# Five of six late transpose groups of a one-core trunk layer: VectorE's 32x32 blocks and a round trip through memory in place of TensorE

## The reference

```python
mod = c_act @ w_ada[l] + b_ada[l]
shift, scale, gate = jnp.split(mod, 3, axis=-1)
h = rms_norm(x, norm_g[l]) * (1 + scale[:, None]) + shift[:, None]
proj = h @ w_in[l]
...
y_pool = multiscale_pool(pool_u, pool_w[l], pool_scale[l]) * jax.nn.silu(pool_z)
y_attn = window_attention(...) * jax.nn.silu(attn_z)
y_conv = conformer_conv(conv_a, conv_b, ..., conv_pw[l]) * jax.nn.silu(conv_z)
g_pool, g_attn, g_conv = jnp.split(jax.nn.sigmoid(gates), 3, axis=-1)
merged = (g_pool * (y_pool @ w_branch_pool[l])
          + g_attn * (y_attn @ w_branch_attn[l])
          + g_conv * (y_conv @ w_branch_conv[l]))
x = x + gate[:, None] * (merged @ w_out[l])
return rms_norm(x, final_g)
```

## Time and profile before

| | |
|---|---|
| median of the runs | 943.31 us |
| span of the profiled execution | 941.5 us |
| PE busy | 910.7 us, 97% of the span |
| DVE busy | 702.5 us, 75% |
| ACT busy | 420.3 us, 45% |
| POOL busy | 9.2 us, 1% |
| HBM read, written | 217.24 MB, 2.10 MB |

### The profile page before, as it was taken

How to read it: one execution, slowest core, us unless ns; L and a number is a source line. 1 busy time by engine, 2 the same in 40 slices (tenths; PEclk the granted TensorE clock), 3 DMA queues, 4 the chain that set the end, 5 groups by cost and what they waited for, 6 DMA issues and landing times.

```text
span 941.5 us, 10294 instructions
## 1 busy us (share of the span) xinstructions
PE 910.7 (97%) x4211; PEld 732.5 (78%) x4211; DVE 702.5 (75%) x793; ACT 420.3 (45%) x387; POOL 9.2 (1%) x26
## 2 busy tenths in 40 slices
PE   1999999999999999999999999999999999999996
PEld 1668677888888888888877777888888888888885
DVE  4768796878968777767778786685687988865783
ACT  3435252645344334444375655447434443444332
POOL 2000000000000000000000000000000000000000
PEclk9999999999999999999999999999999999999999
DMA  9999999855446556555545456657879998965512
GB/s 339 387 387 386 374 328 387 317 182 179 150 161 208 198 181 200 201 179 179 181 136 175 138 157 148 207 172 155 267 242 396 374 335 275 352 209 190 182 45 89
DMA packets 108207, 220.01 MB, mean 234 GB/s; under 512 B 3857, under 2 KB 3937, under 8 KB 107392
## 3 DMA queue, kind: packets, MB, share of 16 engines
q1 hardware_dynamic: 106768, 213.15, 66.6%
q0 software_dynamic: 1104, 5.42, 1.5%
q10 hardware_dynamic: 288, 0.79, 0.2%
HBM read 217.24 MB, written 2.10 MB: 233 GB/s over the span
## 4 chain that ended last, share of the span: by engine, by line
PE 87%; DVE 5%; DMA 4%; ACT 2%; issue 1%; SPq 0%; DVEq 0%; ACTq 0%
PE acc_odd L1245 12%; PE acc_odd L1247 12%; PE acc_odd L1246 12%; PE acc_even L1245 12%; PE acc_even L1247 12%; PE acc_even L1246 12%; DMA raw<-in_w_in 2%; PE side_a L1245 2%; PE side_a L1247 2%; PE side_a L1246 2%; DVE gate_sums L1088 1%; DMA x_tok<-in_x 1%; PE side_b L1294 1%; DVE ada_sums L804 1%; DVE wl L758 1%
## 5 line engine op out<-in xcount | busy, mean ns | idle before, releaser
L758 DVE TENSOR_TENSOR wl<-raw,wh 128x2048 fp32r<-128x2048 f32 x148 | 338.2, 2289 | 148.3 <-ACT wh L466 147.9
L466 ACT ACTIVATE wh<-raw 128x2048 fp32r<-128x2048 f32 x148 | 282.0, 1913 | 263.9 <-PE acc_odd L1247 105.5
L1245 PE MATMUL acc_even<-wh,act_h 128*128 128x512 f32 x432 | 170.5, 395 | 0.6 <-DVE act_l L853 0.6
L1245 PE MATMUL acc_odd<-wh,act_h 128*128 128x512 f32 x432 | 169.8, 393 | 0.0
L1247 PE MATMUL acc_even<-wh,act_l 128*128 128x512 f32 x432 | 168.3, 390 | 0.0
L1246 PE MATMUL acc_odd<-wl,act_h 128*128 128x512 f32 x432 | 168.2, 389 | 0.0
L1247 PE MATMUL acc_odd<-wh,act_l 128*128 128x512 f32 x432 | 168.2, 389 | 0.0
L1246 PE MATMUL acc_even<-wl,act_h 128*128 128x512 f32 x432 | 168.2, 389 | 0.0
L973 DVE SCALAR_TENSOR_TENSOR conv_slots<-conv_slots,taps 128x256 f32<-128x256 f32 x240 | 100.2, 478 | 0.2
L1245 PEld LDWEIGHTS acc_even<-wh,act_h 128*128 128x128 f32 x432 | 81.1, 188 | 20.5 <-issue 3.8
L1245 PEld LDWEIGHTS acc_odd<-wh,act_h 128*128 128x128 f32 x432 | 81.1, 188 | 18.9 <-issue 2.2
(11 more groups left out here) (288 smaller groups left out, 916.8 us busy)
## 6 DMA issues: line engine op xcount, KB each, us to landing
raw<-in_w_in SPq DMA_DIRECT2D x106, 1024.0 KB, 5.1
raw<-in_w_ada SPq DMA_DIRECT2D x48, 1024.0 KB, 8.9
raw<-in_w_out SPq DMA_DIRECT2D x16, 1024.0 KB, 5.0
raw<-in_w_branch_pool SPq DMA_DIRECT2D x8, 1024.0 KB, 5.0
raw<-in_w_branch_attn SPq DMA_DIRECT2D x16, 512.0 KB, 6.7
raw<-in_w_branch_conv SPq DMA_DIRECT2D x8, 1024.0 KB, 6.5
raw<-in_conv_pw SPq DMA_DIRECT2D x4, 1024.0 KB, 6.6
x_tok<-in_x SPq DMA_DIRECT2D x2, 1024.0 KB, 9.0
```

The lines of the kernel that those rows point to most:

```text
L466: nc.scalar.activation(wh[:, m % RING], raw[SLOT_OF[g]][:, :, :], ACT.Copy).then_inc(high_done, 1)
L758: nc.vector.tensor_tensor(wl[:, m % RING], raw[SLOT_OF[load_of(m)]][:, :, :], wh[:, m % RING].bitcast(F32), ALU.subtract).then_inc(raw_don ...
L1245: nc.tensor.matmul(sums, xh, wh[:, slot, i, :], start=begin, stop=False)
```

## The change

Five groups leave PE: both of `zs_conv` and the first three of `merged`. For each, `turn_blocks` on DVE transposes the 32x32 blocks inside each partition quadrant with two instructions of 512 columns, into one of two `blocks` buffers. POOL's `turn` then writes the group to DRAM with four DMAs (one for each quadrant of 32 partitions, 128 KB in 1024 pieces of 128 bytes, 512 bytes apart), waits until all four have landed, and reads it back with two DMAs of 256 KB in rows of 2 KB, into the place where the group came from. ACT's spread and DVE's low_halves then read that place in place of a PSUM bank. The sixth group, `merged` 3, is still turned on PE at m = 137.

What else moves: the spreads of `zs_conv` from m = 111 and 113 to 115 and 116, their low halves from 112 and 114 to 116 and 117; the spread of `merged` 2 from 135 to 136 and its low half to 137; the additions to `gate_rows` from 116 to 121 for the first; the gate row's PSUM place alternates between the two halves of `pa`, so PE waits for the addition before the last one only. On POOL, x_res comes after the first two turns, gate_rows waits for the second low half, and final_rows comes after the last turn, since it lies over `blocks`. Transposes on VectorE and writes to DRAM of such short pieces do not occur in the kernel before.

```diff
--- before.py
+++ after.py
@@ constants and buffers @@
+TURNS = 5
...
+    blocks = [at(f"blocks{s}", [P, 4, 4, TH, QUAD], F32, (176 + 4 * s) * KB) for s in range(2)]
+    scratch = [nc.dram_tensor(f"turned_{g}", (QUAD, 4, 4 * TH, 4, QUAD), F32, kind="Internal").ap() for g in range(TURNS)]
...
+        def turned_tiles(g):
+            return by_channels(g) if g >= 2 else zs_conv[g][:, :, :].rearrange("p h (t s) -> p (h t) s", t=2)
...
+        def by_channels(g):
+            if g < 2:
+                return zs_conv[g][:, :, :].rearrange("p h c -> p (h c)").rearrange("p (q t s) -> p q t s", q=2, t=2)
+            return merged[:, :, bass.ts(g - 2, COLS)].rearrange("p q (t s) -> p q t s", t=2)
@@ gpsimd @@
-            pool.wait_ge(used, END["pw1"])
+            def turn(g):
+
+                pool.wait_ge(blocks_ready, g + 1)
+                for a_ in range(4):
+                    pool.dma_start(scratch[g].rearrange("j b n a i -> j (b n) a i")[:, :, a_, :],
+                                   blocks[g % 2][QUAD * a_:QUAD * (a_ + 1), :, :, :, :].rearrange("j b t h i -> j (b t h) i")
+                                   ).then_inc(blocks_stored, 16)
+                pool.wait_ge(blocks_stored, 16 * 4 * (g + 1))
+                rows = scratch[g].rearrange("j b (q n) a i -> q b j (n a i)", q=2)
+                for q in range(2):
+                    pool.dma_start(by_channels(g)[:, q, :, :].rearrange("p t s -> p (t s)"), rows[q]
+                                   ).then_inc(turned[g], 16)
+
+            turn(0)
+            turn(1)
             pool.dma_start(x_res[:, :, :], x_rows).then_inc(x_res_loaded, 16)
-            pool.dma_start(final_rows[:, :], a["final_g"].partition_broadcast(P)).then_inc(final_loaded, 16)
-            pool.wait_ge(y_t, 4)
+            pool.wait_ge(y_ready, 6)
             pool.dma_start(gate_rows[:, :], a["b_ada"][0, 2 * D_MODEL:3 * D_MODEL].partition_broadcast(P)
                            ).then_inc(gate_b_loaded, 16)
+            for g in range(2, TURNS):
+                turn(g)
+            pool.dma_start(final_rows[:, :], a["final_g"].partition_broadcast(P)).then_inc(final_loaded, 16)
@@ scalar @@
-                if m in (111, 113):
-                    b = (m - 111) // 2
-                    spread(y_h[:, 4 * b:4 * b + 4, :], by_tiles((pa, pb)[b]), y_t, 3 + b, y_high)
+                if m in (115, 116):
+                    b = m - 115
+                    spread(y_h[:, 4 * b:4 * b + 4, :], turned_tiles(b), turned[b], 16 * 2, y_high)
...
-                if m in (131, 133, 135, 137):
-                    j = (m - 131) // 2
-                    spread(act_h[:, 4 * j:4 * j + 4, :], by_tiles((pb, pb, pa, pb)[j]), y_t, 5 + j, y_high)
+                if m in (131, 133, 136):
+                    j = (131, 133, 136).index(m)
+                    act.wait_ge(used, END["gc3"])
+                    spread(high_tiles(j), turned_tiles(2 + j), turned[2 + j], 16 * 2, y_high)
+                if m == 137:
+                    spread(act_h[:, 12:16, :], by_tiles(pb), y_t, 3, y_high)
@@ vector @@
+            def turn_blocks(g, src):
+
+                for h in range(TH):
+                    last = nc.vector.transpose(blocks[g % 2][:, :, :, h, :].rearrange("p b t i -> p t b i"),
+                                               src[:, h, :].rearrange("p (t b j) -> p t b j", t=4, b=4))
+                last.then_inc(blocks_ready, 1)
...
-                if m in (112, 114):
-                    b = (m - 112) // 2
-                    low_halves(5 + b, y_h[:, 4 * b:4 * b + 4, :], y_l[:, 4 * b:4 * b + 4, :], (pa, pb)[b])
+                if m == 112:
+                    for b in range(2):
+                        dve.wait_ge(*freed(f"pw{b}"))
+                        turn_blocks(b, zs_conv[b][:, :, :])
+                if m in (116, 117):
+                    b = m - 116
+                    low_halves(5 + b, y_h[:, 4 * b:4 * b + 4, :], y_l[:, 4 * b:4 * b + 4, :], turned_tiles(b))
+                if m in (122, 124, 134):
+                    j = (122, 124, 134).index(m)
+                    dve.wait_ge(merged_ready, 9 + j)
+                    turn_blocks(2 + j, merged[:, :, bass.ts(j, COLS)])
...
-                if m in (116, 122, 128, 134):
-                    q = (m - 116) // 6
+                if m in (121, 122, 128, 134):
+                    q = (121, 122, 128, 134).index(m)
...
-                if m in (131, 133, 135, 137):
-                    j = (m - 131) // 2
-                    tiles = slice(4 * j, 4 * j + 4)
-                    low_halves(7 + j, act_h[:, tiles, :], act_l[:, tiles, :], (pb, pb, pa, pb)[j])
+                if m in (131, 133, 137):
+                    j = (131, 133, 137).index(m)
+                    low_halves(7 + j, high_tiles(j), low_tiles(j), turned_tiles(2 + j))
+                if m == 137:
+                    low_halves(10, act_h[:, 12:16, :], act_l[:, 12:16, :], by_tiles(pb))
@@ tensor @@
-                if m in (111, 113):
-                    b = (m - 111) // 2
-                    pe.wait_ge(*freed(f"pw{b}"))
-                    if b:
-                        pe.wait_ge(y_ready, 4)
-                    else:
-                        pe.wait_ge(var_ready, 2)
-                    transpose4((pa, pb)[b], block_of(zs_conv[b]), y_t)
                 if m in (114, 120, 126, 132):
                     q = (m - 114) // 6
                     pe.wait_ge(sums_low, q + 1)
...
-                if m in (131, 133, 135, 137):
-                    j = (m - 131) // 2
-                    pe.wait_ge(merged_ready, 9 + j)
...
-                    transpose4((pb, pb, pa, pb)[j], block_of(merged, COLS * j), y_t)
+                if m == 137:
+                    pe.wait_ge(merged_ready, 12)
+                    pe.wait_ge(y_ready, 4)
+                    transpose4(pb, block_of(merged, COLS * 3), y_t)
```

30 lines of the change are left out of this document (16 added, 14 removed).

## The result

The changed kernel takes **968.85 us** (median of 4 runs, 967.50 to 971.56), the kernel before 943.25 beside it: ratio 1.0273, 95% interval 1.0261 to 1.0285, 25.6 us slower. The forecast was 955.8 (946.5 to 980). The profiled execution took 967.5.

A forecast was written before the change was run, and what follows sets the result against it. PE was taken as the bound, busy 910.7 of 941.5 us. The terms 0 + 6.2 + 2.8 - 2.6 + 6.1 gave +12.5 us on 943.3, so 955.8 us, range 946.5 to 980.

The forecast's parts named there:

- (c): DMA, m = 112 to 120: full engines, short write pieces at three times their bytes' time; second gate row +6.2 us.
- (e): Last turned group, o0's third piece: write phase 9.6, reads 4.4, then 6.6 to the operand; PE stands for 6.1 us.
- (a): On PE's path: five transpose groups leave, 5 x 0.88 = 4.4 us; first two lie ahead of the first gate row.
- (b): DVE at m = 112: four transposes add 2.6 us, `gate_low` starts as before, PE waits 1.8 longer; net 0.
- (d): DVE between gate rows, m = 120 and 126: transposes and moved addition delay third `gate_low`, +2.8 us; later DMAs cost nothing.
- (f): Moved x_res (some 40 us later) and final_rows: cost nothing, hidden by o0; SP's queue not touched, only its bandwidth.
- sum of the low bounds: Whole kernel: every term at its low bound but (b), +3.8 - 0.9, given as about +4 us.
- short-piece rival: Round-trip writes: 1024 pieces take pool_w's time whatever their bytes, 16 us a group; +27, 970.6 us; chance 0.33.

The follow-up runs named there:

- tiny: Changed kernel with the round trip's DMAs cut to a quarter of their bytes each way, most turned values left out: 951.90 us.
- tinyx: Changed kernel with the round trip's DMAs cut to a quarter of their bytes each way and x_res loaded behind the last turn: 944.56 us.
- xlate: Changed kernel with the load of x_res moved behind the last turn, just ahead of final_rows: 966.88 us.
- long2: Changed kernel with the round trip's writes in pieces of 4 KB in place of 128 bytes, values ending at other places: 964.89 us.
- reads16: Changed kernel with each group's read-back cut into four DMAs by partitions in place of two by halves: 966.94 us.
- both5: Changed kernel with read-backs in four DMAs by partitions and x_res loaded behind the last turn: 958.05 us.

## Why the prediction was right and wrong

The sign and the place of the waits were right, and the time lay in the range; the size was half of what came. Most of the miss is in (c), in (e) and in a term for the clock that the sum doesn't have.

(a), (b) *Right.* PE lost the groups; a transpose took 0.65 from start to start as taken, the first gate row waits 1.4 (forecast 1.8), net -0.7 for 0; the gate sums came 1.9 earlier (711.52 for 713.44) where I took 1.5.

(c) **The step that failed**, by its size and by its reason. +9.3 for +6.2. I had put it on the short pieces of the writes, at three times their bytes. Long pieces change this stretch by nothing (42.9 for 42.5), unless the two causes I had left out are gone: reads slow by their form, and x_res, which I had kept in the same sum as before because its bytes were in the stretch anyway. They weren't at the same place in it: before, x_res was issued at 707.8, in the changed kernel at 737.6, just when the weights for the second gate row were due, and by tiny and tinyx that costs 5.5 us. And I added the terms, where the runs show that each late load hides the others. The way in was in my text, though only under a rival: ACT in front of the copy of group 1.

(d) *Right in its own size, short of its consequence.* The third gate row waits 2.27 for the 2.8 forecast, unchanged with most of the DMA's bytes gone (tinyx). The other 2.9 of that stretch are the clock, a term that was missing here and in (e): I read 1.00 in the stretch as a constant, though I was adding waits to it. The sentence that the later groups' DMAs cost nothing was wrong by 1.6 us, the wait for the fourth gate row. PE's wait alone can mislead there, since PE comes 1.6 later wherever the clock fell behind the third row. DVE's `gate_low` tells it: from its third to its fourth end pass 35.0 us in the changed kernel, 35.1 in xlate and 34.5 in long2, but 32.9 in reads16, 32.8 in both5 and 32.9 in tinyx. So it goes with the slow reads at their full size, not with x_res.

(e) *The mechanism right, one term mis-sized.* The write phase took 8.8 for 9.6, from landing to PE 6.4 for 6.6. The reads took 8.6 for 4.4: I had priced them by an output DMA of 384 KB, with full rows on both sides, and looked at their bytes alone. Wait 9.8 for 6.1, and 1.5 of clock behind it.

(f) *Half wrong.* Nobody missed x_res or final_rows late, as said; x_res left POOL 30 us later, not 40. That x_res cost nothing where it now stands was wrong, as under (c).

The sum of the low bounds was wrong as well: 0.8 + 1.3 - 2.6 + 2.6 is +2.1, and +1.2 with (b) at -0.9, not about +4.

*The short-piece rival* gave 970.6, within 2 us of the result, and that is luck: its writes of 16 us a group took 6 to 11. It had +14.6 for the second gate row where +9.3 came, and a wait of 12.5 at the third piece where 9.8 came; what it had too much there stands for the clock and the fourth row, which it lacks. At the last group the short pieces took 8.8 where its rule had 15.7 and long pieces took 4.5. The Trainium skill ("DMA: Bandwidth & Descriptors", Specifications) has transfers under 512 B read, modified and written; that they cost more here the traces show, in what way they don't. The Trainium skill's advice weighed under (b) ("VectorE: DVE Perf Modes", Rules for kernel authors: TensorE wherever a PSUM destination will do) agrees with the trace: 1.30 us for a group's two transposes on DVE, 0.88 on PE.

## What to carry to other kernels

Moving work off the bounding engine gave nothing where the engine that took it had no slack ahead of the same wait: compare 0.88 us saved with 1.3 paid, before asking about DMA. Price a DMA by its form as well as its bytes (how the transfer is cut into DMAs, the shortest piece), look for the loads that it will run beside, and ask what stands in line behind whoever waits for it: moving that consumer back by two steps gave 5.6 us for an edit of two numbers. When several things make one wait late, removing one shows little; change them in combination before calling any of them innocent, and count the clock behind each wait that you add.
